# A causal convolution's taps: eight of 31 on TensorE, or fourteen of 31 on GpSimd

## The chip, the cores and the metric

The kernel runs on one core of one Trainium2 chip. The metric is the device time of one execution in microseconds; of several executions the median is given.

## What is computed

Two stacked networks on 256 tokens of width 1024, in float32. The first has two layers of SwiGLU and mixer (pooling, then latent attention); the second has a mixer of three branches and a mixture of experts. The change touches the second network's mixer:

```python
o_a = dsa_attention(q_a, k_a, v_a, q_i, k_i, w_i, topk)              # 8 heads
o_b = conformer_conv(conv_in, conv_w[l], conv_b[l], ln_g[l], ln_b[l])
o_m = memory_attention(q_m, mem, g_mem[l], w_mem_kv[l], g_qm[l], g_km[l])   # 4 heads
merged = (gates[:, :, 0] * (o_a @ w_br_a[l]) + gates[:, :, 1] * (o_b @ w_br_b[l])
          + gates[:, :, 2] * (o_m @ w_br_m[l]))
x = x + merged @ w_o[l]

def conformer_conv(conv_in, conv_w, conv_b, ln_g, ln_b):
    a, gte = jnp.split(conv_in, 2, axis=-1)
    u = a * jax.nn.sigmoid(gte)                       # (256, 512)
    y = depthwise causal convolution of u, 31 taps, + conv_b
    return jax.nn.silu(layernorm(y, ln_g, ln_b))
```

## The kernel before

The program is written out by hand for five engines, and its order is the order of the code; semaphores join the engines. Weights stream from HBM in blocks of 128 rows into a ring `raw`. Each block is split in two parts of reduced precision, `uh` on ScalarE (L449) and `ul = raw - uh` on VectorE (L460), and TensorE multiplies each block three times (L524 to L526), once with each useful pair of parts. The activations are split alike into `hh`/`hl` or `bh`/`bl`.

Steps of other work are put between the blocks: `later` holds generators that give a step at each `unit_done`, by a budget; `flush` runs what is left. So the heads of the two attentions run beside the gates' blocks: eight heads `qa`, then four heads `qm`. A head is turned, scored, its maximum taken on VectorE (`heads_dve`, L1783 or L1787), its exponential on ScalarE (L1754), then turned and multiplied (L1702, L1715). `heads_dve` calls `extra` once per step, and `extra` issues four taps of the convolution.

The convolution works on columns: `uT` holds `u` turned, 4 groups of 128 channels by 286 positions, 30 of them zeros, copied from PSUM at L2596. The tap (k, j) is `uT[:, k, j:j+256]` times the column `cw[:, k, j]`. `cw` comes at L2681, from the rows that GpSimd loads as `conv_w`. The taps 0 to 22 of each group, 92 in all, are VectorE's: one instruction of 128x256 each (L2390 for the first, L2392 for the others) that adds into `yc`. All `arena` and `Gs` names in the rows of this line are SBUF tiles. The taps 23 to 30, 32 in all, are TensorE's: ScalarE makes a diagonal matrix from the identity and the tap's column (`taps_act`, L2400), and TensorE multiplies two 128x128 pieces of `uT` by it and adds up in two banks (`taps_pe`, L2409). Each of these float32 products is two records in the trace. Then TensorE adds `yc`, turned by a product with the identity (L2553), into the same banks. VectorE takes mean and variance (L2731, L2733), ScalarE and VectorE make the root (L802, L791 to L797), and VectorE writes the normed rows (L2740).

Around that stand the three branches (`branch_pe`). A branch has two column halves c of four input blocks k each. Branch 0 takes `o_a`, then branch 2 takes `o_m` (turned at L837, parts at L852 and L858), then branch 1 takes the convolution. Merges are on VectorE (L2488). The order on TensorE is: branch 0, flush of the heads `qm`, eight of its taps, the turn of `om`, 24 taps, the sum with `yc`, branch 2 with the turn of the normed rows at the start of its second half, branch 1.

GpSimd makes loads of its own queue (L3344, L691), the roots of some norms (L998, L1000), the division in the latent attention's softmax (L1956) and four small rows (L1584). After the load of `conv_w` it waits for the heads' end and issues eight loads for the router.

## Time and profile before

| | us |
|---|---|
| median of 3 runs (lowest, highest) | 1565.17 (1562.39, 1565.42) |
| the profiled execution, its own time | 1564.39 |
| its span in the profile | 1562.3 |
| TensorE busy | 1523.4 (98%) |
| VectorE busy | 1217.6 (78%) |
| ScalarE busy | 877.4 (56%) |
| GpSimd busy | 117.2 (8%) |
| DMA, mean share of 16 engines | 373.75 MB at 239 GB/s |

The span is that of the profiled execution; 2.1 us of its time lie around it. "PE" in the rows is TensorE's products, "PEld" its weight loads, "DVE" VectorE, "ACT" ScalarE, "POOL" GpSimd. Products overlap, so the step from one start to the next tells what a row of products costs, not the duration of one. In a timeline row, `x4` with a time means four instructions in a row within that time.

### The profile page before, as it was taken

What the parts mean: (1) busy time and instruction counts of PE and PEld (TensorE: products, weight loads), DVE (VectorE), ACT (ScalarE), POOL (GpSimd) and SP (SyncE); (2) the same over time, 40 slices, a digit from 0 to 9 for tenths busy, and PEclk for the clock granted to TensorE, in tenths of its full rate; (3) what the DMA queues carried; (4) which work ended last, traced back from release to release, by engine and by line L of the source; (5) the groups of instructions that cost most, each with busy time, mean ns of one, the idle gap of its engine ahead of it and who ended that gap; (6) DMA issues with size and microseconds to landing.
All of it is one profiled execution on the core that took longest, in us unless ns stands there. A gap on an engine that the chain in (4) does not pass through costs nothing.

```text
span 1562.3 us, 19111 instructions
## 1 busy us (share of the span) xinstructions
PE 1523.4 (98%) x7361; PEld 1218.0 (78%) x7361; DVE 1217.6 (78%) x1782; ACT 877.4 (56%) x1349; POOL 117.2 (8%) x180
## 2 busy tenths in 40 slices
PE   7999999999999999999999999999999999999997
PEld 4878876878878887766788887877788888787876
DVE  1898978988868888665585654669888798888996
ACT  2545436544447444377564544655567477777774
POOL 1110020000001000015211000000001000000000
PEclk9999999999999999999999999899999999999999
DMA  9999856988857988333286544445324479989893
GB/s 345 374 378 357 301 202 217 333 301 305 305 178 264 339 285 309 118 109 108 82 310 189 185 147 142 157 152 193 113 81 131 162 258 363 344 316 334 306 344 132
DMA packets 196400, 373.75 MB, mean 239 GB/s; under 512 B 9042, under 2 KB 102672, under 8 KB 196304
## 3 DMA queue, kind: packets, MB, share of 16 engines
q1 hardware_dynamic: 176688, 301.08, 55.8%
q0 software_dynamic: 18928, 69.77, 12.7%
q10 hardware_dynamic: 688, 1.62, 0.3%
q8 instruction: 60, 0.98, 0.2%
q14 instruction: 36, 0.29, 0.1%
HBM read 371.39 MB, written 1.05 MB: 238 GB/s over the span
## 4 chain that ended last, share of the span: by engine, by line
PE 89%; ACT 4%; DVE 4%; POOL 1%; DMA 1%; SPq 1%; issue 1%; DVEq 0%; ACTq 0%
PE banks L524 25%; PE banks L526 25%; PE banks L525 25%; PE banks L1165 1%; ACT arena L807 1%; ACT uh L449 1%; DVE ul L460 1%; PE banks L2409 1%; DMA raw<-in_ffn_w_in 1%; PE banks L3011 1%; PE banks L835 1%; PE banks L981 1%; PE banks L2018 1%; PE banks L1843 1%; PE banks L766 1%
## 5 line engine op out<-in xcount | busy, mean ns | idle before, releaser
L460 DVE TENSOR_TENSOR ul<-raw,uh 128x1024 fp32r<-128x1024 f32 (+2 forms) x548 | 657.1, 1209 | 156.3 <-ACT uh L449 147.2
L449 ACT ACTIVATE uh<-raw 128x1024 fp32r<-128x1024 f32 (+2 forms) x548 | 568.4, 1048 | 346.7 <-PE banks L526 342.4
L524 PE MATMUL banks<-uh,hh 128*128 128x512 f32 (+2 forms) x1296 | 517.4, 399 | 4.2 <-DVE ul L460 1.9
L526 PE MATMUL banks<-uh,hl 128*128 128x512 f32 (+2 forms) x1296 | 503.9, 389 | 0.0
L525 PE MATMUL banks<-ul,hh 128*128 128x512 f32 (+2 forms) x1296 | 503.0, 388 | 0.0
L524 PEld LDWEIGHTS banks<-uh,hh 128*128 128x128 f32 x1296 | 245.5, 189 | 60.3 <-issue 6.1
L526 PEld LDWEIGHTS banks<-uh,hl 128*128 128x128 f32 x1296 | 245.3, 189 | 51.1
L525 PEld LDWEIGHTS banks<-ul,hh 128*128 128x128 f32 x1296 | 245.9, 190 | 45.4 <-issue 0.2
L524 PE MATMUL banks<-uh,bh 128*128 128x512 f32 x512 | 207.3, 405 | 1.0 <-DVE bl L3208 0.9
L526 PE MATMUL banks<-uh,bl 128*128 128x512 f32 x512 | 200.0, 391 | 0.0
L525 PE MATMUL banks<-ul,bh 128*128 128x512 f32 x512 | 199.5, 390 | 0.0
L715 DVE SCALAR_TENSOR_TENSOR arena<-arena,sc 128x512 f32<-128x512 f32 x210 | 157.9, 752 | 9.9 <-DVE bl L1233 0.5
L524 PEld LDWEIGHTS banks<-uh,bh 128*128 128x128 f32 x512 | 96.1, 188 | 29.2 <-DVE bl L3208 6.2
L526 PEld LDWEIGHTS banks<-uh,bl 128*128 128x128 f32 x512 | 96.1, 188 | 20.9
L525 PEld LDWEIGHTS banks<-ul,bh 128*128 128x128 f32 x512 | 96.3, 188 | 20.0 <-issue 1.7
L691 POOL DMA_DIRECT2D arena<-in_ada_w x60 | 45.3, 755 | 472.5 <-DVE arena L715 397.9
L1215 ACT ACTIVATE sg<-banks 128x256 f32<-128x256 f32 x88 | 29.0, 380 | 62.0 <-PE banks L526 62.0
L2392 DVE SCALAR_TENSOR_TENSOR Gs<-arena,Gs 128x256 f32<-128x256 f32 x88 | 42.7, 485 | 3.2
L1248 DVE TENSOR_TENSOR ug<-sg,banks 128x256 f32<-128x256 f32 x88 | 33.0, 415 | 11.4 <-ACT sg L1215 11.3
L1233 DVE TENSOR_TENSOR bl<-banks,bh 128x512 fp32r<-128x512 f32 x44 | 30.1, 684 | 4.1 <-ACT bh L1203 4.1
L774 ACT ACTIVATE arena<-banks 128x128 f32<-128x128 f32 x20 | 5.6, 279 | 40.6 <-PE banks L751 40.6
L1203 ACT ACTIVATE bh<-banks 128x512 fp32r<-128x512 f32 x44 | 25.6, 582 | 4.3 <-PE banks L1165 4.3
(402 smaller groups left out, 1267.0 us busy)
## 6 DMA issues: line engine op xcount, KB each, us to landing
raw<-in_ffn_w_in SPq DMA_DIRECT2D x176, 512.0 KB, 6.7
raw<-in_w_up SPq DMA_DIRECT2D x64, 1024.0 KB, 6.5
arena<-in_ada_w POOLq DMA_DIRECT2D x60, 1024.0 KB, 7.4
raw<-in_ffn_w_out SPq DMA_DIRECT2D x44, 1024.0 KB, 5.7
raw<-in_w_down SPq DMA_DIRECT2D x32, 1024.0 KB, 6.2
raw<-in_w_in SPq DMA_DIRECT2D x22, 1024.0 KB, 5.0
raw<-in_ada_w SPq DMA_DIRECT2D x12, 1024.0 KB, 10.5
raw<-in_w_mem_kv SPq DMA_DIRECT2D x4, 1024.0 KB, 6.0
```

The costliest lines, as they stand in the source:

```text
L449: act.e.activation(uh[r][:, 0:w], raw[m % NRAW][:, h * w:(h + 1) * w], AF.Copy).then_inc(act_done, ta.put("hi", u))
L460: dve.e.tensor_tensor(ul[r][:, 0:w], raw[m % NRAW][:, h * w:(h + 1) * w], uh[r][:, 0:w].bitcast(F32), ALU.subtract).then_inc(dve_done, tv. ...
L524: pe.e.matmul(o, a, wh, start=k + j == s0, stop=False)
L525: pe.e.matmul(o, a, wl, start=False, stop=False)
L526: mm = pe.e.matmul(o, b, wh, start=False, stop=k + j == s1)
L691: pool.e.dma_start(ada_raw[m % NADA], v).then_inc(ada_ring[m % NADA], 16)
L715: dve.e.scalar_tensor_tensor(buf, w, sc[:, k:k + 1], buf, ALU.mult, ALU.add).then_inc(dve_done, tv.put())
L1203: act.e.activation(gT_h[b % 2][:, :, :], PB[6][:, :].rearrange("p (a b) -> p a b", b=S), AF.Copy).then_inc(act_done, ta.put("gh", q, b))
L1215: act.e.activation(sg[:, t, :], PB[up_banks(b)[t]][:, 0:256], AF.Silu).then_inc(act_done, ta.put("silu", q, b, t))
L1233: dve.e.tensor_tensor(gT_l[n][:, :, :], PB[6][:, :].rearrange("p (a b) -> p a b", b=S), gT_h[n][:, :, :].bitcast(F32), ALU.subtract).then_inc(
L1248: mul = dve.e.tensor_tensor(o, sg[:, t, :], u, ALU.mult)
L2392: tap = dve.e.scalar_tensor_tensor(y, u, w, y, ALU.mult, ALU.add)
```

## The change

GpSimd makes the taps 17 to 30 of each group (56), VectorE the taps 0 to 16 (68), and TensorE and ScalarE none. On GpSimd a tap is a product into `pt` (TENSOR_SCALAR) and an addition into `py` (TENSOR_TENSOR); the first four products go to `py` itself, so there are 56 products and 52 additions. Three products are issued ahead, and a product waits for the addition four places earlier in its buffer. VectorE adds `py` to `yc` (`taps_sum_dve`), and TensorE turns the sum into the two banks inside branch 0, before block 2 of its second half. The norm's root moves to GpSimd, by a power of -0.5. GpSimd's loads for the router stand behind that. The two new tiles take 8 KB of each partition, and the scratch for GpSimd's descriptors shrinks to 8192 bytes.

```diff
-PE_TAPS = 8
+POOL_TAPS = 14
+        py = sb("py", [P, 4, S])
+        pt = sb("pt", [P, 4, S])
...
-        def taps_act(act, taps, n):
...
-        def taps_pe(pe, taps, n):
...
+        def taps_pool(pool):
+            def product(i):
+                k, j = POOL_LIST[i]
+                o = py[:, k, :] if i < 4 else pt[:, i % 4, :]
                 if i >= 8:
+                    pool.wait_ge(pool_done, tg("tap", i - 4))
+                pool.e.tensor_scalar(o, uT[:, k, j:j + S], cw[:, k, j:j + 1], None, ALU.mult).then_inc(
+                    pool_done, tg.put("product", i))
+
+            pool.wait_ge(dve_done, tv("cw"))
+            pool.wait_ge(act_done, ta("uT", 2))
+            n = len(POOL_LIST)
+            for i in range(7):
+                product(i)
+            for i in range(4, n):
+                if i + 3 < n:
+                    product(i + 3)
+                y = py[:, i % 4, :]
+                pool.wait_ge(pool_done, tg("product", i))
+                if i < 8:
+                    pool.wait_ge(pool_done, tg("product", i - 4))
+                else:
+                    pool.wait_ge(pool_done, tg("tap", i - 4))
+                pool.e.tensor_tensor(y, y, pt[:, i % 4, :], ALU.add).then_inc(pool_done, tg.put("tap", i))
+
+        def taps_sum_dve(dve):
+            last = len(POOL_LIST) - 4
+            for k in range(4):
+                dve.wait_ge(pool_done, tg("tap", last + k))
+                dve.own()
+                dve.e.tensor_tensor(yc[:, k, :], yc[:, k, :], py[:, k, :], ALU.add).then_inc(
+                    dve_done, tv.put("conv", k))
...
+            def conv_out():
+                pe.later.flush("qm")
+                tp.same("ht")
...
+                for k in range(4):
+                    pe.wait_ge(dve_done, tv("conv", k))
+                    for t in range(T):
+                        mm = pe.e.transpose(PB[6 + t][:, k * P:(k + 1) * P], yc[:, k, t * P:(t + 1) * P], ident[:, :])
+                mm.then_inc(pe_done, tp.put("conv"))
...
+            branch_pe(pe, 0, lbh, lbl, parts_ready(pe, "oa"), mids={(1, 2): conv_out})
             turn_pe(pe, "om", 4, om_part, lambda: pe.wait_ge(dve_done, tv("o", "qm", 1, 0)))
-            taps_pe(pe, taps, 999)
...
-            act.wait_ge(dve_done, tv("ss", "ln"))
-            rstd_act(act, "ln", st[:, 50:52], 1)
...
+            merge_dve(dve, 0, 0)
+            dve.unit_done()
+            taps_dve(dve, taps, 999)
+            taps_sum_dve(dve)
+            split_low(dve, dve.unit_at + 1)
+            dve.unit_done()
+            dve.unit_done()
             dve.later.flush("qm")
             tv.same("ht")
-            taps_dve(dve, taps, 6)
-            split_low(dve, dve.unit_at + 3)
+            merge_dve(dve, 0, 1)
             plain_dve(dve, "om", 4, bh, bl)
-            taps_dve(dve, taps, 999)
             dve.wait_ge(pe_done, tp("conv"))
...
+            split_low(dve, dve.unit_at + 3)
+            for t in range(T):
+                dve.wait_ge(pool_done, tg("lnr", t))
...
             load("conv_w", cwr, I["conv_w_2"][0].rearrange("j a n -> j (a n)"))
+            taps_pool(pool)
+            for t in range(T):
+                r = st[:, 52 + t:53 + t]
+                pool.wait_ge(dve_done, tv("ss", "ln", t))
+                pool.e.tensor_scalar(r, st[:, 41 + 2 * t:42 + 2 * t], EPS, None, ALU.add).then_inc(pool_done, tg.put())
+                pool.wait_ge(pool_done, tg.n)
+                pool.e.tensor_tensor(r, r, minus_half, ALU.pow).then_inc(pool_done, tg.put("lnr", t))
...
-    nc = _bacc.Bacc("TRN2", target_bir_lowering=False, num_devices=1)
+    nc = _bacc.Bacc("TRN2", target_bir_lowering=False, num_devices=1, dynamic_dma_scratch_size=8192)
```

The lines of the changed kernel stand one further down up to 2390 or so, and about ten from there on. TensorE before, from the last step of the heads to the first product of branch 2; L524 to L526 are branch products, L1715 a head, L2409 the taps, L837 the turn of `om`, L2553 the sum:

```order
L1715 MATMUL banks<-kvm,Gs 128x128 x4
L524 MATMUL banks<-uh,bh 128x512
...
L526 MATMUL banks<-uh,bl 128x512
L2409 MATMUL banks<-arena 128x128 x16
L837 MATMUL banks<-ident,arena 128x128 x8
L2409 MATMUL banks<-arena 128x128 x48
L2553 MATMUL banks<-ident,Gs 128x128 x8
L524 MATMUL banks<-uh,bh 128x512
```

The same place now; L2567 is the turn of the sum:

```order
L1716 MATMUL banks<-kvm,Gs 128x128 x4
L2567 MATMUL banks<-ident,Gs 128x128 x8
L525 MATMUL banks<-uh,bh 128x512
...
L527 MATMUL banks<-uh,bl 128x512
L838 MATMUL banks<-ident,arena 128x128 x8
L525 MATMUL banks<-uh,bh 128x512
```

The taps are gone, and the sum stands in front of the last twelve products of branch 0 instead of behind the turn.

VectorE before, from the last head to the norm; L1787 and L1792 are a head's maximum, L2392 taps, L2488 a merge, L1798 and L1804 the heads' end, L858 low parts of `om`:

```order
L1787 TENSOR_REDUCE st<-banks 128x2
L1792 SCALAR_TENSOR_TENSOR st<-st 128x2
L2392 SCALAR_TENSOR_TENSOR Gs<-arena,Gs 128x256 x4
L2488 TENSOR_TENSOR arena<-arena,banks 128x512 x2
L2392 SCALAR_TENSOR_TENSOR Gs<-arena,Gs 128x256 x8
L2488 TENSOR_TENSOR arena<-arena,banks 128x512 x2
L1798 RECIPROCAL st<-st 128x8
L1804 TENSOR_TENSOR arena<-banks,st 128x512 x2
L2392 SCALAR_TENSOR_TENSOR Gs<-arena,Gs 128x256 x6
L460 TENSOR_TENSOR ul<-raw,uh 128x1024 x3
L858 TENSOR_TENSOR bl<-banks,bh 128x512 x2
L2392 SCALAR_TENSOR_TENSOR Gs<-arena,Gs 128x256 x14
```

Now; L2426 is the sum with GpSimd's taps, L2745 to L2751 the norm:

```order
L2393 SCALAR_TENSOR_TENSOR Gs<-arena,Gs 128x256 x4
L2503 TENSOR_TENSOR arena<-arena,banks 128x512 x2
L2393 SCALAR_TENSOR_TENSOR Gs<-arena,Gs 128x256 x4
L2426 TENSOR_TENSOR Gs<-Gs,py 128x256 x4
L461 TENSOR_TENSOR ul<-raw,uh 128x1024
L1799 RECIPROCAL st<-st 128x8
L1805 TENSOR_TENSOR arena<-banks,st 128x512 x2
L2503 TENSOR_TENSOR arena<-arena,banks 128x512 x2
L859 TENSOR_TENSOR bl<-banks,bh 128x512 x2
L2745 BN_STATS st<-banks 128x6
L2747 BN_AGGR st<-st 128x2
```

Of these 32 taps 24 are gone, four stay in front of the first merge and four behind it, and the four sums stand before the second merge. Two splits (L461) follow the statistics, ahead of the normed rows. GpSimd now, behind its load of the tap weights (before, the loads for the router came next):

```order
L3355 DMA arena<-in_conv_w 31x512
L2402 TENSOR_SCALAR py<-arena 128x256 x4
L2402 TENSOR_SCALAR pt<-arena 128x256 x4
L2419 TENSOR_TENSOR py<-py,pt 128x256
L2402 TENSOR_SCALAR pt<-arena 128x256
```

The last two rows then alternate up to the last four additions.

## Rows read from the trace of the kernel before

**Rows 1.** The page: busy time and share, and the chain by engine.
```profile
PE 1523.4 (98%) x7361; PEld 1218.0 (78%) x7361; DVE 1217.6 (78%) x1782; ACT 877.4 (56%) x1349; POOL 117.2 (8%) x180
...
PE 89%; ACT 4%; DVE 4%; POOL 1%; DMA 1%; SPq 1%; issue 1%; DVEq 0%; ACTq 0%
```

**Rows 2.** Busy time by stretches: from the tap weights to the sum's new place.
```profile
core 0: us, PE busy (x) PEld busy (x) DVE busy (x) ACT busy (x) POOL busy (x), PEclk, DMA share, GB/s
1073.50:1171.00 97.50, 96.85 (x502) 77.79 (x502) 83.99 (x158) 60.17 (x120) 0.00 (x0) 1.00 0.36 119
```

**Rows 3.** TensorE's timeline: start, us in all, what [idle before].
```profile
1170.95 0.48 PE L524 MATMUL banks<-uh,bh 128*128 128x512 f32 x1
...
1173.77 3.73 PE L2409 MATMUL banks<-arena 128*128 128x128 f32 x32
1177.34 1.04 PE L837 MATMUL banks<-ident,arena 128*128 128x128 f32 x8
1179.40 10.98 PE L2409 MATMUL banks<-arena 128*128 128x128 f32 x96 [1.03 <-ACT arena L2400]
1190.33 2.27 PE L2553 MATMUL banks<-ident,Gs 128*128 128x128 f32 x16
1192.36 0.48 PE L524 MATMUL banks<-uh,bh 128*128 128x512 f32 x1
...
1197.91 1.03 PE L837 MATMUL banks<-ident,arena 128*128 128x128 f32 x8
```

**Rows 4.** ScalarE's timeline: the turned input, and the parts of `om`.
```profile
1069.92 1.07 ACT L2596 ACTIVATE arena<-banks 128x512 f32<-128x512 f32 x2
...
1177.98 1.09 ACT L852 ACTIVATE bh<-banks 128x512 fp32r<-128x512 f32 x2 [5.52 <-PE banks L837]
```

**Rows 5.** VectorE's timeline: the tap weights, the last taps, the norm, the router's weights.
```profile
1073.16 0.28 DVE L2681 COPY arena<-banks 128x124 f32<-128x124 f32 x1
...
1167.68 4.13 DVE L2392 SCALAR_TENSOR_TENSOR Gs<-arena,Gs 128x256 f32<-128x256 f32 x8
...
1195.98 1.53 DVE L2740 TENSOR_SCALAR arena<-banks,st 128x512 f32<-128x512 f32 x2
...
1233.05 0.45 DVE L2757 TENSOR_TENSOR arena<-arena,cc 128x288 f32<-128x288 f32 x1
```

**Rows 6.** VectorE's timeline at two places of the first network.
```profile
477.40 0.42 DVE L1096 TENSOR_TENSOR hl<-full,hh 128x256 fp32r<-128x256 f32 x1
477.74 1.22 DVE L460 TENSOR_TENSOR ul<-raw,uh 128x1024 fp32r<-128x1024 f32 x1
...
676.01 1.02 DVE L460 TENSOR_TENSOR ul<-raw,uh 128x832 fp32r<-128x832 f32 x1
```

**Rows 7.** GpSimd's groups by form: busy us, mean ns | idle before.
```profile
L1956 POOL TENSOR_SCALAR full<-full,st 128x256 f32<-128x256 f32 x16 | 14.6, 925 | 7.5 <-DVE st L1923 7.5
...
L1584 POOL TENSOR_TENSOR arena<-arena 4x256 f32<-4x256 f32 x2 | 1.5, 730 | 1.4 <-DMA arena<-in_pool_scale 1.3
```

**Rows 8.** GpSimd's timeline: the norms' roots, and the first load for the router.
```profile
468.00 0.30 POOL L998 TENSOR_SCALAR st<-st 128x1 f32<-128x1 f32 x1 [47.10 <-ACT arena L807]
468.39 0.57 POOL L1000 TENSOR_TENSOR st<-st 128x1 f32<-128x1 f32 x1
...
478.50 0.63 POOL L998 TENSOR_SCALAR st<-st 128x1 f32<-128x1 f32 x1 [3.56 <-ACT arena L807]
...
676.76 0.43 POOL L998 TENSOR_SCALAR st<-st 128x1 f32<-128x1 f32 x1 [3.56 <-ACT arena L807]
...
1177.42 0.55 POOL L3344 DMA_DIRECT2D Gs<-in_g_ffn  x1 [196.86 <-DVE Gs L2392]
```

**Rows 9.** VectorE's groups by form from 1073.5 to 1171 us.
```profile
L2392 DVE SCALAR_TENSOR_TENSOR Gs<-arena,Gs 128x256 f32<-128x256 f32 x67 | 32.5, 485 | 2.4
L460 DVE TENSOR_TENSOR ul<-raw,uh 128x1024 fp32r<-128x1024 f32 x21 | 25.4, 1222 | 6.8 <-ACT uh L449 6.5
...
L1636 DVE TENSOR_TENSOR Gs<-arena 128x320 f32<-128x320 f32 x2 | 1.0, 494 | 0.1
```

More of the change, by code:

```diff
@@ L370, in build @@
         cwr = om[0:CONVW, 0, :]
-        dg = [v[:, t, h * P:(h + 1) * P] for v in (mask, score) for t in range(T) for h in range(2)]
         grow = ht
@@ L2393, in taps_dve @@
                 tap.then_inc(dve_done, tv.put("tap", k, j))
-        def taps_act(act, taps, n):
-            for i, (k, j) in taps.some(n):
-                act.wait_ge(dve_done, tv("o", "qa", 1, 0))
+        def taps_pool(pool):
+            def product(i):
+                k, j = POOL_LIST[i]
+                o = py[:, k, :] if i < 4 else pt[:, i % 4, :]
                 if i >= 8:
-                    act.wait_ge(pe_done, tp("tap", i - 8))
-                act.e.activation(dg[i % 8], ident[:, :], AF.Copy, scale=cw[:, k, j:j + 1]).then_inc(
-                    act_done, ta.put("dg", i))
-        def taps_pe(pe, taps, n):
-            for i, (k, j) in taps.some(n):
-                pe.wait_ge(act_done, ta("dg", i))
-                for t in range(T):
-                    if i == 0:
-                        pe.take(6 + t)
-                    mm = pe.e.matmul(PB[6 + t][:, k * P:(k + 1) * P], uT[:, k, j + t * P:j + (t + 1) * P], dg[i % 8],
-                                     start=(i == 0), stop=False)
-                mm.then_inc(pe_done, tp.put("tap", i))
+                    pool.wait_ge(pool_done, tg("tap", i - 4))
[23 more added lines that the diff above has]
+                    dve_done, tv.put("conv", k))
         gsel, gbias = gb[:, 512:518], gb[:, 0:512]
@@ L2542, in mix_pe @@
                 pe, "oa", 4, om_part, lambda: pe.wait_ge(dve_done, tv("o", "qa", 1, 0)), bk=OA_BANKS))
-            branch_pe(pe, 0, lbh, lbl, parts_ready(pe, "oa"))
-            pe.later.flush("qm")
-            tp.same("ht")
-            taps = Taps(PE_LIST)
-            taps_pe(pe, taps, 8)
-            turn_pe(pe, "om", 4, om_part, lambda: pe.wait_ge(dve_done, tv("o", "qm", 1, 0)))
-            taps_pe(pe, taps, 999)
-            for k in range(4):
-                pe.wait_ge(dve_done, tv("tap", k, CONVW - PE_TAPS - 1))
-                for t in range(T):
-                    mm = pe.e.matmul(PB[6 + t][:, k * P:(k + 1) * P], yc[:, k, t * P:(t + 1) * P], ident[:, :],
-                                     start=False, stop=(k == 3))
-            mm.then_inc(pe_done, tp.put("conv"))
-            for t in range(T):
-                pe.frees(6 + t, dve_done, tv, "ln", t)
+            def conv_out():
+                pe.later.flush("qm")
+                tp.same("ht")
+                for t in range(T):
+                    pe.take(6 + t)
+                for k in range(4):
[4 more added lines that the diff above has]
+                for t in range(T):
+                    pe.frees(6 + t, dve_done, tv, "ln", t)
+            branch_pe(pe, 0, lbh, lbl, parts_ready(pe, "oa"), mids={(1, 2): conv_out})
+            turn_pe(pe, "om", 4, om_part, lambda: pe.wait_ge(dve_done, tv("o", "qm", 1, 0)))
             def ln_turn():
```

21 lines of the change are left out of this document (6 added, 15 removed).

## The prediction

> **What bounds the kernel now.** I read the page first. TensorE is busy for 98% of the span and GpSimd for 8%, and TensorE holds 89% of the chain that ended last [rows 1]. So time is won where TensorE has fewer instructions on that chain, and lost where it is made to wait. Then I read the table by stretches for the part that the change touches. Between 1073.5 us, when the turned tap weights are there, and 1171 us, when TensorE has done two of the four input blocks of the second half of branch 0, TensorE is busy for 96.85 of 97.5 us, VectorE for 83.99, ScalarE for 60.17, and GpSimd not at all; the granted clock is 1.00, TensorE's upper level of 2.4 GHz [rows 2]. TensorE sets the pace there, and VectorE has 13.5 us to spare. Third, TensorE's timeline: behind branch 0 come 32 tap products from 1173.77, the turn of `om`, a wait, 96 tap products from 1179.40, the 16 products of the sum, and branch 2 from 1192.36 [rows 3]. Last, I looked at what GpSimd and VectorE do to each other, since the change puts the two beside each other.
>
> **What the change takes from TensorE.** The 32 PE taps (two matmuls each, shown as 128 records) go. Start to start they take 1177.34 - 1173.77 = 3.57 us and 1190.33 - 1179.40 = 10.93 us: 14.5 us [rows 3], all on the path. The sum's products stay (1192.36 - 1190.33 = 2.0 us), moved into branch 0. The idle time in front of 1179.40 (1.0 us) is replaced by a wait for the high parts of `om`: ScalarE makes them in 1.09 us from 1177.98, right behind the turn [rows 4]. Branch 2 now stands there, so I count that as even. ScalarE also loses 32 products and, with the root, a table load: it idled 5.52 us before those high parts [rows 4], so this is worth nothing. From TensorE alone: **-14.5 us**.
>
> **What VectorE must do by then.** Its 68 taps are as many as it had done in the heads before: 4 first taps, then four per head step, and the four that I take from the group of eight that starts at 1167.68 [rows 5]; they end at 1167.68 + 4 x 0.516 (4.13 / 8) = 1169.75. New are four sums, 0.42 us each by a 256 wide addition [rows 6], so the sum is ready at about 1171.4, and TensorE, there at 1170.95 [rows 3], waits 0.5 to 1 us: **+0.7 us**. The 24 taps that VectorE loses (12.4 us) stood beside the 96 products and were not on the path. They are worth nothing.
>
> **GpSimd's own work.** The inputs are there early: the turned rows at 1069.92 + 1.07 us [rows 4], the weights at 1073.16 + 0.28 = 1073.44 [rows 5]. GpSimd then issues 56 products and 52 additions of 128x256. A product is a TENSOR_SCALAR of that very size, 0.925 us; the nearest addition row is a TENSOR_TENSOR of 4x256, 0.730 us [rows 7]. The program has a wait for the addition in front of nearly every product, and such a step costs 0.39 - 0.30 = 0.09 us [rows 8]. With 56 x 0.925 + 52 x (0.73 + 0.09) = 51.8 + 42.6 I get **94 us**: alone it would be done at 1167.8, before VectorE's last tap. If nothing disturbs it, it is hidden.
>
> **The disturbance.** Here the trace speaks against the change. A 128x1 TENSOR_SCALAR on GpSimd takes 0.30 us (468.00). Twice it was longer in the rows shown (and once more, alike, at 781): 0.63 us from 478.50 and 0.43 from 676.76 [rows 8]. Each time VectorE was in the split L460, which reads `raw` and `uh`, both in SBUF: until 478.96 and 677.03 [rows 6]. GpSimd ended at 479.13 and 677.19, so each time 0.16 or 0.17 us behind VectorE's end. That isn't a share of a bandwidth; GpSimd stood still until VectorE was through. Of the reverse, VectorE held by a reading GpSimd, the trace has no case: VectorE has no instruction with two SBUF inputs beside the 32 products of 0.92 us in the latent attention [rows 7]. I take it that the wait goes both ways, because what makes one of two engines wait for the other's whole instruction is most simply one thing that either can hold.
>
> Price: 0.30 us of a GpSimd instruction is there even for one column [rows 8], so a product reads for 0.925 - 0.30 = 0.625 us and an addition for 0.43. In all 56 x 0.625 + 52 x 0.43 = 57 us, 0.53 on average. VectorE's instructions with two SBUF inputs in the stretch are 67 taps (32.5 us), 21 splits (25.4), 12 steps of the rotation (six lines like the one shown, 6.0) and 3 short ones for the norms (1.3): 103 instructions, 65 us [rows 9]. VectorE's other 19 us cover about 19 / 0.83 = 22 GpSimd instructions. The other 86 each push VectorE back by 0.53 us: 46 us. VectorE's 13.5 us of spare time take up a part, so it ends 32 us late. One GpSimd instruction for each of VectorE's also means that GpSimd ends no later than VectorE. TensorE needs VectorE in every head (the maxima) and for every split, and has 0.65 us of idle time: it is late by the same **+32 us**. Bounds: if everything packs perfectly, 65 + 57 = 122 us have to fit in 97.5, which is +25; if an instruction holds for its whole length, 65 + 90 = 155, which is +57. I take 32, since the 0.30 us row is GpSimd's own overhead and is near.
>
> The Trainium skill, page "SBUF — State Buffer", section "Who interferes with whom", has a rule on just this: a VectorE instruction with two SBUF inputs contends with a GpSimd instruction that reads SBUF, and whichever starts first holds the shared ports for its whole instruction. The held rows agree with it in one direction, and no row here shows the other. By that rule to the letter the wait would be the upper bound, +57, and the sum +44.
>
> **Behind the sum.** The norm's root moves to GpSimd: 0.30 + 0.57 us per row block plus the step between (0.09) [rows 8], in place of ScalarE's table load and VectorE's four small steps. From the sum's end TensorE has 2.8 us of branch 0, 0.9 of the turn, 1.1 of waiting and 5.5 of branch 2 (1197.91 - 1192.36 [rows 3]) before it wants the normed rows, 10.3 us. VectorE needs until then a merge, low parts, two statistics, two splits and the two normings (1.53 us [rows 5]): about 11.3 us. **+1.0 us**. GpSimd's eight loads for the router now stand behind the roots. They took 5 us to issue from 1177.42 [rows 8] and are wanted at 1233 [rows 5]; even 40 us of lateness shifts both alike. The smaller descriptor scratch I cost at nothing, since GpSimd sits idle before nearly every load; if that cover fails, a load starts a few us later in the first half of the kernel.
>
> **Sum.** -14.5 + 0.7 + 32 + 1.0 = +19.2 us on the profiled execution's 1564.39: 1583.6. The median of the runs is 0.8 above the profiled one, so I forecast **1584 us**. With the bounds of the wait, 1577 (+25) to 1609 (+57).
>
> **Rivals.** (a) No disturbance: GpSimd is done at 1167.8 and only -14.5 + 0.7 + 1.0 = -12.8 remains, 1552. For it: no row shows VectorE held. Against it: the held instructions [rows 8]. Faster. (b) Only GpSimd waits, VectorE never: behind each VectorE instruction it gets one in, and with waits of about 0.2 us in each of 103 it ends some 20 us after 1167.8, so TensorE waits about 16 us at the sum: +3, 1568. For it: the rows show just this direction. The point from which it decides is a GpSimd end after 1171 with VectorE on time. (c) VectorE always goes first and GpSimd gets only the remainder, 97.5 - 65 = 32 us, or 39 instructions; the other 69 take 59 us alone, so TensorE waits at one place until 1230: +59 - 13 = +46, 1611. (d) The change doesn't do what it says: the order of instructions shows that it does, so no chance of its own.
>
> **Numbers.** Forecast 0.5, (a) 0.27, (b) 0.13, (c) 0.1. Since (a) is above 0.2 the range must hold it; it leaves out (c) and the top of the forecast's own bounds: 1551 to 1602. The likeliest case's own range is 1577 to 1609. 0.2%, some 3 us, is about what a measurement of this kernel can tell from no change: faster is (a) and a little of (b), 0.28; the same is half of (b), 0.08; slower is the rest, 0.64.
>
> **What would show it.** L2393 and L461 on VectorE, 485 and 1222 ns now, get longer or get idle time in front of them by about half a us each; the 56 products average above 925 ns; the stretch from the weights to the sum lasts about 130 us instead of 97.5; TensorE's busy share in it falls to about three quarters, with waits spread over all heads. Right behind it 14.5 us are gone. If VectorE's means stay and GpSimd ends before TensorE reaches the sum, (a) is right and I am wrong in the disturbance; one long wait of TensorE before L2567 would be (b) or (c).

## The result and the profile after

| | before, measured beside it | after |
|---|---|---|
| median, us (lowest, highest) | 1564.09 (1562.37, 1565.42) | 1574.26 (1572.48, 1576.81) |
| ratio (95% interval) | | 1.0073 (1.0062 to 1.0084) |
| profiled execution, own time / span | 1564.39 / 1562.3 | 1576.81 / 1575.2 |

Slower by 10.2 us, where 19.2 were forecast. The profiled execution of after is the slowest of its six, so differences of spans (12.9) are some 3 us above those of medians.

The page of after, busy time and chain by engine, answers to [rows 1]:

```profile
PE 1513.7 (96%) x7225; PEld 1206.4 (77%) x7225; DVE 1222.2 (78%) x1756; ACT 866.4 (55%) x1315; POOL 236.2 (15%) x292
...
PE 80%; POOL 8%; DVE 5%; ACT 3%; issue 1%; DMA 1%; SPq 1%; DVEq 0%; ACTq 0%
```

GpSimd had 1% of the chain and now has 8%; TensorE fell from 89 to 80. So the path went over to GpSimd somewhere. The table by stretches answers to [rows 2]: first from the tap weights (1074.50) to the end of the heads, then two stretches behind TensorE's wait:

```profile
1074.50:1178.00 103.50, 98.58 (x501) 78.72 (x501) 96.86 (x155) 59.30 (x113) 99.45 (x88) 0.98 0.33 112
...
1193.40:1196.00 2.60, 2.19 (x8) 1.17 (x9) 2.30 (x4) 0.00 (x0) 1.44 (x2) 0.50 0.00 0
1196.00:1200.00 4.00, 4.00 (x16) 3.23 (x15) 2.19 (x4) 0.00 (x0) 0.00 (x0) 0.73 0.53 156
```

In the first row VectorE is busy for 96.86 us, where it was 83.99, and TensorE still for 95% of the time: the heads are 5.8 us longer (TensorE is at the sum 103.3 us after the weights instead of 97.5), not 32. The granted clock is 0.50 behind the wait, TensorE's lower level of 1.2 GHz. TensorE's timeline, answering to [rows 3]:

```profile
1177.03 1.05 PE L1716 MATMUL banks<-kvm,Gs 128*128 128x128 f32 x8
1193.44 0.69 PE L2567 MATMUL banks<-ident,Gs 128*128 128x128 f32 x2 [15.37 <-DVE Gs L2426]
1194.31 0.69 PE L2567 MATMUL banks<-ident,Gs 128*128 128x128 f32 x2 [0.18 <-DVE Gs L2426]
...
1199.86 1.03 PE L838 MATMUL banks<-ident,arena 128*128 128x128 f32 x8
...
1202.13 0.50 PE L525 MATMUL banks<-uh,bh 128*128 128x512 f32 x1 [1.23 <-DVE bl L859]
```

One wait of 15.4 us before the sum. Who is late is told by VectorE's timeline, answering to [rows 5]:

```profile
1174.81 2.43 DVE L2393 SCALAR_TENSOR_TENSOR Gs<-arena,Gs 128x256 f32<-128x256 f32 x4
1192.46 3.19 DVE L2426 TENSOR_TENSOR Gs<-Gs,py 128x256 f32<-128x256 f32 x4 [15.22 <-POOL py L2419]
...
1204.49 2.33 DVE L461 TENSOR_TENSOR ul<-raw,uh 128x1024 fp32r<-128x1024 f32 x2
1206.73 1.52 DVE L2751 TENSOR_SCALAR arena<-banks,st 128x512 f32<-128x512 f32 x2
```

VectorE is through with its taps at 1177.24 and idles for 15.2 us, released by GpSimd's addition. GpSimd's timeline from there, with the roots of the norm:

```profile
1189.10 0.92 POOL L2402 TENSOR_SCALAR pt<-arena 128x256 f32<-128x256 f32 x1
1189.99 0.72 POOL L2419 TENSOR_TENSOR py<-py,pt 128x256 f32<-128x256 f32 x1
1190.81 0.92 POOL L2402 TENSOR_SCALAR pt<-arena 128x256 f32<-128x256 f32 x1
1191.70 3.13 POOL L2419 TENSOR_TENSOR py<-py,pt 128x256 f32<-128x256 f32 x4
1203.71 0.22 POOL L3425 TENSOR_SCALAR st<-st 128x1 f32<-128x1 f32 x1 [8.88 <-DVE st L2747]
1204.02 0.57 POOL L3427 TENSOR_TENSOR st<-st 128x1 f32<-128x1 f32 x1
1204.67 1.09 POOL L3425 TENSOR_SCALAR st<-st 128x1 f32<-128x1 f32 x1
1205.84 1.38 POOL L3427 TENSOR_TENSOR st<-st 128x1 f32<-128x1 f32 x1
```

GpSimd worked from 1074.61 to 1194.84: 120.2 us where I had 94. The second pair of roots takes 1.09 and 1.38 us instead of 0.22 and 0.57; it stands beside the two splits of 1204.49. Last the groups, VectorE's to 1178 answering to [rows 9], GpSimd's to [rows 7]:

```profile
L2393 DVE SCALAR_TENSOR_TENSOR Gs<-arena,Gs 128x256 f32<-128x256 f32 x64 | 41.6, 650 | 2.3
L461 DVE TENSOR_TENSOR ul<-raw,uh 128x1024 fp32r<-128x1024 f32 x21 | 26.1, 1254 | 0.9 <-ACT uh L450 0.9
...
L1793 DVE SCALAR_TENSOR_TENSOR st<-st 128x2 f32<-128x2 f32 x12 | 3.4, 287 | 0.4
...
L2391 DVE TENSOR_SCALAR Gs<-arena,cc 128x256 f32<-128x256 f32 x4 | 2.4, 590 | 0.1
```

```profile
L2402 POOL TENSOR_SCALAR pt<-arena 128x256 f32<-128x256 f32 x52 | 62.8, 1209 | 4.7
L2419 POOL TENSOR_TENSOR py<-py,pt 128x256 f32<-128x256 f32 x52 | 48.1, 928 | 0.0
L2402 POOL TENSOR_SCALAR py<-arena 128x256 f32<-128x256 f32 x4 | 6.1, 1539 | 93.1 <-DVE arena L2692 93.1
```

Both engines are held by the other: a tap on VectorE went from 485 to 650 ns, a product on GpSimd from 925 to 1233 (68.9 us / 56), an addition from 0.72 (its length behind 1178, with VectorE idle) to 928.

Where the 12.9 us between the spans are: tap weights later +1.1 (in runs 1 and 3 below, with the same code up to there, they are ready at 1070.6, so this is scatter of the first network), heads +5.8, from their end to the sum +15.6 (the wait), taps of TensorE -14.5, the rest up to branch 2 (the half clock, the handing over of `om`) +1.8, branch 2 to the turn in its middle +0.9, behind it +2.2.

### The profile page after: what moved, and what is told of

Its sections match the earlier page's. It is cut to its first block, busy times and chain, and to the rows that moved or that the text cites. A ratio compares the mean times of both kernels' runs of the same rounds, so it can differ in the third digit from the quotient of the medians.

```text
span 1575.2 us, 18895 instructions
## 1 busy us (share of the span) xinstructions
PE 1513.7 (96%) x7225; PEld 1206.4 (77%) x7225; DVE 1222.2 (78%) x1756; ACT 866.4 (55%) x1315; POOL 236.2 (15%) x292
## 3 DMA queue, kind: packets, MB, share of 16 engines
HBM read 371.39 MB, written 1.05 MB: 236 GB/s over the span
## 4 chain that ended last, share of the span: by engine, by line
PE 80%; POOL 8%; DVE 5%; ACT 3%; issue 1%; DMA 1%; SPq 1%; DVEq 0%; ACTq 0%
PE banks L525 24%; PE banks L527 23%; PE banks L526 23%; POOL pt L2402 4%; POOL py L2419 3%; DVE ul L461 2%; PE banks L1166 1%; ACT arena L808 1%; ACT uh L450 1%; DMA raw<-in_ffn_w_in 1%; PE banks L3022 1%; PE banks L836 1%; PE banks L982 1%; PE banks L2019 1%; PE banks L1844 1%
## 5 line engine op out<-in xcount | busy, mean ns | idle before, releaser
L461 DVE TENSOR_TENSOR ul<-raw,uh 128x1024 fp32r<-128x1024 f32 (+2 forms) x548 | 658.0, 1211 | 150.1 <-ACT uh L450 141.6
L526 PE MATMUL banks<-ul,hh 128*128 128x512 f32 (+2 forms) x1296 | 504.5, 389 | 0.0
L526 PEld LDWEIGHTS banks<-ul,hh 128*128 128x128 f32 x1296 | 246.8, 190 | 45.7 <-issue 0.2
L526 PE MATMUL banks<-ul,bh 128*128 128x512 f32 x512 | 200.0, 391 | 0.0
L526 PEld LDWEIGHTS banks<-ul,bh 128*128 128x128 f32 x512 | 96.6, 189 | 19.9 <-issue 1.7
L2402 POOL TENSOR_SCALAR pt<-arena 128x256 f32<-128x256 f32 x52 | 62.8, 1209 | 4.7
L2419 POOL TENSOR_TENSOR py<-py,pt 128x256 f32<-128x256 f32 x52 | 48.1, 928 | 0.0
L999 POOL TENSOR_SCALAR st<-st 128x1 f32<-128x1 f32 x16 | 5.5, 347 | 268.1 <-ACT arena L808 268.1
```

The lines of the kernel that those rows point to most:

```text
L461: dve.e.tensor_tensor(ul[r][:, 0:w], raw[m % NRAW][:, h * w:(h + 1) * w], uh[r][:, 0:w].bitcast(F32), ALU.subtract).then_inc(dve_done, tv. ...
L526: pe.e.matmul(o, a, wl, start=False, stop=False)
L2402: pool.e.tensor_scalar(o, uT[:, k, j:j + S], cw[:, k, j:j + 1], None, ALU.mult).then_inc(pool_done, tg.put("product", i))
L2419: pool.e.tensor_tensor(y, y, pt[:, i % 4, :], ALU.add).then_inc(pool_done, tg.put("tap", i))
```

## The experiments

The time of each run is compared with the kernel before as measured beside that run (medians of 1561.8 to 1563.2 us), and two runs are compared by their differences from it. In runs 1, 2, 3, 5 and 6 the result of the convolution is incomplete or wrong, since GpSimd's share is left out or replaced.

Theory when they began: VectorE and GpSimd hold each other (but for less than forecast), and GpSimd's late end makes the wait. Rival: GpSimd is just slow, or something else in the changed order is.

**1. GpSimd's taps left out**

```diff
-            taps_pool(pool)
...
-                dve.wait_ge(pool_done, tg("tap", last + k))
...
-                dve.e.tensor_tensor(yc[:, k, :], yc[:, k, :], py[:, k, :], ALU.add).then_inc(
+                dve.e.tensor_tensor(yc[:, k, :], yc[:, k, :], yc[:, k, :], ALU.max).then_inc(
```

> GpSimd's 108 instructions are left out, and the four sums on VectorE take the maximum of yc with itself, so the result lacks the taps 17 to 30; all else is the changed kernel. Theory (the two engines hold each other up at a shared read of SBUF, and the sum then waits for GpSimd): with no GpSimd work VectorE's taps take 485 ns again, the splits 1222, TensorE reaches the sum 6 us sooner and doesn't wait 15 us there: 1574 - 6 - 15 = 1553 us, which is also the 1552 that I gave for no disturbance. Rival (the loss lies in the new order: the sum inside branch 0, the norm's root on GpSimd behind its own queue): the sum's 15 us go, but VectorE's 6 us of lateness stay: 1559 us or more.

Measured: 1547.78 us, 0.9911 (0.9894 to 0.9928) of before, 5 us below the expectation. VectorE's groups have their old lengths:

```profile
L2393 DVE SCALAR_TENSOR_TENSOR Gs<-arena,Gs 128x256 f32<-128x256 f32 x64 | 31.0, 485 | 2.3
L461 DVE TENSOR_TENSOR ul<-raw,uh 128x1024 fp32r<-128x1024 f32 x25 | 30.2, 1221 | 6.8 <-ACT uh L450 6.6
```

TensorE's timeline at the sum shows no wait, 97.6 us after the weights (1070.57):

```profile
1168.15 1.04 PE L2566 MATMUL banks<-ident,Gs 128*128 128x128 f32 x8
...
1171.77 1.03 PE L838 MATMUL banks<-ident,arena 128*128 128x128 f32 x8
```

So everything that the change costs comes from GpSimd's 108 instructions and the wait for them: 10.2 us above the kernel before with them, 15.4 below it without, 25.6 in all. It also shows a price that I did not have: from the sum to the turn of `om` it is 3.6 us here and 6.4 in the changed kernel (1193.44 to 1199.86), where the granted clock is 0.50 and 0.73, against 1.00 here. The wait costs TensorE 2.8 us more than its own length; 0.4 of them are two more short waits, and the other 2.4 go with the lower clock.

**2. GpSimd works, nobody waits for it at the sum.** As 1, but with `taps_pool`.

> GpSimd makes all its 108 instructions, but the four sums on VectorE don't read or await them (they take the maximum of yc with itself), so the result lacks the taps 17 to 30. Theory: the disturbance stays and only the wait at the sum goes. VectorE's taps keep their 650 ns mean in the heads, TensorE is about 6 us late there, and the norm's root on GpSimd now has to queue behind the unfinished taps: GpSimd's end stays near 1194 us, the roots come behind it, and the turn of the normed rows waits for them, about 10 us. So 1574 - 15 + 5 to 10 = 1564 to 1569 us. Rival (VectorE is not held by GpSimd but by something in the order of its own work): GpSimd's instructions are as long as alone (0.92 and 0.73 us) once nothing waits for them.

Measured: 1568.04 us, 1.003 (1.0018 to 1.0041). The groups are as in the changed kernel (taps 651 ns), and TensorE is at the sum after 103.4 us. So the 5.8 us in the heads are VectorE's lateness alone, and no effect of the wait. But of the wait's 15.4 us only 5.4 came back in the time (10.2 above the kernel before with it, 4.8 without). TensorE's waits tell why:

```profile
PE banks L838 <- DVE arena L2750: 8.1, 1, 8.1
PE banks L1703 <- ACT Gs L1765: 3.8, 4, 1.5
```

The second line is 3.8 us in the changed kernel too and 0.2 in run 1: it is the lateness in the heads. L2750 is the normed rows, which need the root, and the root stands behind the last addition on GpSimd (1196.63 us there). GpSimd's late end is paid at the next place that needs the engine.

**3. The same number of writes without a read.** Each product and addition becomes a MEMSET of 128x1024 that waits for the one before; the sums wait for the last four, but don't read them.

```diff
-                pool.e.tensor_scalar(o, uT[:, k, j:j + S], cw[:, k, j:j + 1], None, ALU.mult).then_inc(
-                    pool_done, tg.put("product", i))
+                pool.wait_ge(pool_done, tg.n)
+                pool.e.memset((py if i < 4 else pt)[:, :, :], 0.0).then_inc(pool_done, tg.put("product", i))
...
-                pool.e.tensor_tensor(y, y, pt[:, i % 4, :], ALU.add).then_inc(pool_done, tg.put("tap", i))
+                pool.wait_ge(pool_done, tg.n)
+                pool.e.memset(py[:, :, :], 0.0).then_inc(pool_done, tg.put("tap", i))
```

> GpSimd's 56 products and 52 additions are replaced by 108 MEMSETs of 128x1024 into pt and py, each waiting for the one before, and the sums don't read py but still wait for the last four; the result lacks the taps 17 to 30. GpSimd then writes as much as it can and reads nothing. Theory (only a GpSimd instruction that reads SBUF holds up VectorE's second input): VectorE's taps are back at 485 ns and its two-column instruction of a head at 161 ns, while GpSimd is busy beside them. Rival (any GpSimd work, or its writes, holds VectorE up): taps stay above 550 ns and the two-column instruction above 200.

Measured: 1561.32 us (one run). GpSimd is busy for 108 x 0.955 = 103.1 us within 109.3, and VectorE's groups read:

```profile
L2393 DVE SCALAR_TENSOR_TENSOR Gs<-arena,Gs 128x256 f32<-128x256 f32 x64 | 31.0, 485 | 2.3
L461 DVE TENSOR_TENSOR ul<-raw,uh 128x1024 fp32r<-128x1024 f32 x22 | 26.6, 1222 | 6.8 <-ACT uh L450 6.5
...
L2391 DVE TENSOR_SCALAR Gs<-arena,cc 128x256 f32<-128x256 f32 x4 | 4.0, 988 | 0.1
```

A GpSimd that is busy and writes does nothing to taps and splits; the one that makes products and additions does. The four first taps L2391 are the surprise: one input, and 988 ns instead of 414 (run 1) beside writes. The time is still 13.5 us above run 1: TensorE is 1.9 us later at the end of the heads (the four L2391 take 2.3 us more), it waits 7.2 us and three times 0.3 at the sum, because 109.3 us of MEMSETs end behind VectorE's taps, and comes to the turn of `om` 8.3 us after the start of the sum instead of 3.6. A GpSimd chain that is too long costs time without disturbing a tap.

**4. The smaller descriptor scratch alone**, in the kernel before.

```diff
-    nc = _bacc.Bacc("TRN2", target_bir_lowering=False, num_devices=1)
+    nc = _bacc.Bacc("TRN2", target_bir_lowering=False, num_devices=1, dynamic_dma_scratch_size=8192)
```

> The kernel before with nothing changed but the descriptor scratch of 8192 bytes. I costed that at nothing: 1564 us, ratio 1.000 within 0.1%. Rival (GpSimd's loads of the first network start later, which would explain that the changed kernel reaches the tap weights 1.1 us later than the kernel before): +1 us, 1565.

Measured: 1563.02 us, 1.0002 (0.9993 to 1.0012). Nothing, as costed.

**5 and 6. Only one-input, only two-input instructions on GpSimd.** I had priced a hold as the instruction's length less 0.30 us, which makes the product (0.625) worse than the addition (0.43).

```diff
-                pool.e.tensor_tensor(y, y, pt[:, i % 4, :], ALU.add).then_inc(pool_done, tg.put("tap", i))
+                pool.e.tensor_scalar(y, pt[:, i % 4, :], cw[:, 0, 0:1], None, ALU.mult).then_inc(pool_done, tg.put("tap", i))
```

```diff
-                pool.e.tensor_scalar(o, uT[:, k, j:j + S], cw[:, k, j:j + 1], None, ALU.mult).then_inc(
+                pool.e.tensor_tensor(o, uT[:, k, j:j + S], uT[:, k, 0:S], ALU.add).then_inc(
```

> All 108 GpSimd instructions read one array of SBUF (the additions are replaced by the multiplication of the product slot by a scalar, written to the sum; GpSimd's share of the convolution is wrong). My step in the prediction took a hold as an instruction's length less 0.30 us, so products (0.925 us, hold 0.625) would disturb more than additions (0.73 us, hold 0.43): VectorE's taps would have a mean over 650 ns, about 700. Theory now: a product holds VectorE's reads for about 0.2 us only and an addition for 0.5: taps' mean 530 to 590 ns, the two-column instructions near 161, and the sum place of TensorE reached about 100 us after the weights. GpSimd ends later than in the changed kernel either way (108 x 0.93 is 100 us alone, with VectorE's holds 120 to 130).

> All 108 GpSimd instructions read two arrays of SBUF (the products are replaced by additions of two stretches of the input; GpSimd's share is wrong). Theory now: additions hold VectorE for about 0.5 us each and come every 0.8 us: taps' mean 720 to 850 ns, two-column instructions 350 or more, splits over 1270. GpSimd ends about 90 to 100 us after the weights, so that the wait at the sum is under 3 us. Rival (hold is length less 0.30 us, products the worse): taps' mean 600 to 650 ns.

Measured, one run each: 1581.67 and 1575.94 us. The groups to 1178 us, first of only products, then of only additions:

```profile
L2393 DVE SCALAR_TENSOR_TENSOR Gs<-arena,Gs 128x256 f32<-128x256 f32 x64 | 34.2, 534 | 2.3
L461 DVE TENSOR_TENSOR ul<-raw,uh 128x1024 fp32r<-128x1024 f32 x22 | 27.9, 1276 | 4.5 <-ACT uh L450 4.5
```

```profile
L2393 DVE SCALAR_TENSOR_TENSOR Gs<-arena,Gs 128x256 f32<-128x256 f32 x48 | 39.0, 812 | 1.7
L461 DVE TENSOR_TENSOR ul<-raw,uh 128x1024 fp32r<-128x1024 f32 x21 | 34.4, 1650 | 0.0
```

Products cost a tap 49 ns, additions 327: the order is the reverse of mine. And the greater loss goes to the other side in each: with products alone GpSimd needs 128.8 us (104 by its steps of 0.96 us where VectorE is idle) and TensorE waits 27.5 us at the sum; with additions alone GpSimd is done in 104.2 us (89 by the steps of 0.82 us in the changed kernel), and VectorE is so late that the sum comes at 1196.29, with no wait there and TensorE's waits in the heads. So both of the cases that I weighed against each other exist, by the kind of instruction on GpSimd. Of the theory's numbers two were missed: GpSimd's 104.2 us with additions, where 90 to 100 were expected, and VectorE's two-column instructions, 184 ns with products instead of 161. The two kinds differ in two things, the operation and the number of arrays that GpSimd reads, and no run parts them: that it is the second array that makes an addition dear is argued, not shown.

Single collisions can be read from the changed kernel's timelines. Here are rows of GpSimd and VectorE by their starts, in windows narrow enough to hold one instruction:

```profile
1117.10 0.97 POOL L2402 TENSOR_SCALAR pt<-arena 128x256 f32<-128x256 f32 x1
1117.32 0.58 DVE L2393 SCALAR_TENSOR_TENSOR Gs<-arena,Gs 128x256 f32<-128x256 f32 x1
1118.05 0.97 POOL L2419 TENSOR_TENSOR py<-py,pt 128x256 f32<-128x256 f32 x1
1118.46 0.85 DVE L2393 SCALAR_TENSOR_TENSOR Gs<-arena,Gs 128x256 f32<-128x256 f32 x1
1119.12 2.03 POOL L2402 TENSOR_SCALAR pt<-arena 128x256 f32<-128x256 f32 x1
1119.22 1.21 DVE L461 TENSOR_TENSOR ul<-raw,uh 128x1024 fp32r<-128x1024 f32 x1
```

A tap takes 0.485 us undisturbed. The one that starts while a product is under way takes 0.58, the one that starts while an addition is under way 0.85; all 18 taps of that second sort in the changed kernel take 0.83 to 0.85, and in run 5, with products alone, none of the 64 taps takes more than 0.73. The other way round the product of 1119.12 is not done until 0.7 us behind the end of the split (1120.43): it waited for the tap before and for the whole split. The addition of 1118.05 waited for the end of a tap at 1118.42 and ended 0.60 us behind it. So either kind waits for the end of the VectorE instruction that is under way, a product makes the next tap wait for about 0.1 us (0.25 at most in run 5), and an addition for about 0.35. (Four taps of 1.05 us are an exception: an addition that started 0.04 us behind each of them was not held, and the tap was. Why is open.)

**7 and 8. Twelve taps on GpSimd, nineteen on VectorE**; then also the sum behind the turn of `om` (on VectorE the last taps, a split and the four sums move along with it).

```diff
-POOL_TAPS = 14
+POOL_TAPS = 12
```

```diff
-            branch_pe(pe, 0, lbh, lbl, parts_ready(pe, "oa"), mids={(1, 2): conv_out})
+            branch_pe(pe, 0, lbh, lbl, parts_ready(pe, "oa"))
...
             turn_pe(pe, "om", 4, om_part, lambda: pe.wait_ge(dve_done, tv("o", "qm", 1, 0)))
+            conv_out()
```

> GpSimd makes 12 taps, VectorE 19: 16 fewer GpSimd instructions, and 8 more taps on VectorE. Theory (GpSimd is the bound, 120.2 us for 108 instructions, and VectorE's sum place is reached at 1177 in the changed kernel): GpSimd ends 1.1 us x 16 = 18 us earlier, about 1177; VectorE's taps end 8 x 0.6 = 5 us later, about 1182; the sum at about 1183 instead of 1193, time 1564 to 1566. Rival (disturbance of VectorE is the cost, as I predicted, and moves with its load): VectorE with more taps ends later still, and the time stays at 1570 or more.

> As with 12 taps on GpSimd, but the sum stands behind the turn of the memory heads' output on TensorE and on VectorE, so that the last rows of the heads cover the end of the taps. Theory: the wait at the sum shrinks by the 2 to 4 us of the turn, 1560 to 1564. Rival (the sum is on the path wherever it stands, since the turn is short and needs VectorE, which is behind its taps): no better than with 12 taps alone.

Measured: 1562.12 us, 0.9999 (0.999 to 1.0009), and 1561.46, 0.9994 (0.9984 to 1.0004): level with the kernel before. VectorE's timeline with twelve taps:

```profile
1173.76 8.08 DVE L2393 SCALAR_TENSOR_TENSOR Gs<-arena,Gs 128x256 f32<-128x256 f32 x12
1181.95 2.01 DVE L2426 TENSOR_TENSOR Gs<-Gs,py 128x256 f32<-128x256 f32 x4
```

The sums start right behind the taps: GpSimd was done at 1180.5, and now VectorE is the bound; TensorE's wait is 5.4 us. The better balance brings 10.6 us (10.2 above the kernel before, now 0.5 below it), where 8 to 10 were expected. GpSimd's 92 instructions, 80 us without disturbance by the reckoning of the prediction, took 107.0, so it ended 3.5 us later than expected. Run 8 came out inside its expectation, but by its rival: at the later place the wait doesn't shrink, it is 6.5 us, since VectorE comes to the sum only after a merge, two splits and the low parts of `om`, and the 0.7 us between the two runs are inside their scatter.

**9. Two taps back on TensorE**: 12 on GpSimd, 17 on VectorE, the sum late as in 8.

```diff
-POOL_TAPS = 14
+PE_TAPS = 2
+POOL_TAPS = 12
...
-DVE_TAPS = [(k, j) for j in range(CONVW - POOL_TAPS) for k in range(4)]
+DVE_TAPS = [(k, j) for j in range(CONVW - POOL_TAPS - PE_TAPS) for k in range(4)]
+PE_LIST = [(k, j) for j in range(CONVW - POOL_TAPS - PE_TAPS, CONVW - POOL_TAPS) for k in range(4)]
...
+            taps_act(act, Taps(PE_LIST), 8)
...
             def conv_out():
+                taps_pe(pe, Taps(PE_LIST), 999)
```

> 12 taps on GpSimd, 17 on VectorE, 2 on TensorE by diagonal products (the way of the kernel before, 8 diagonal matrices from ScalarE), sum behind the turn of the memory heads' output. Theory (with 12 taps on GpSimd VectorE is the bound: its taps and what stands behind them keep TensorE waiting 6.5 us at the sum): two taps less take 8 x 0.65 = 5 us from VectorE, and the 16 products of TensorE (3.6 us) run inside its wait: the sum can start about 1183 instead of 1187, GpSimd being done at about 1180; 1556 to 1558, the first version under the kernel before by more than 0.2%. Rival (GpSimd's end at 1180, or the products added to TensorE, give it back): 1560 or more.

Measured: **1556.52 us, 0.9964 (0.995 to 0.9978)**, 5.2 us below the kernel before and inside the expectation. TensorE's timeline:

```profile
1178.01 3.74 PE L2413 MATMUL banks<-arena 128*128 128x128 f32 x32
1182.80 2.30 PE L2585 MATMUL banks<-ident,Gs 128*128 128x128 f32 x16 [1.05 <-DVE Gs L2447]
```

The tap products fill what was a wait, and no half clock follows: the granted clock is 1.00 from 1178 to 1190 us.

**10. The splits moved behind the normed rows**, in the changed kernel.

> The changed kernel with the two splits of the next weights moved behind the normed rows, so that nothing of VectorE stands beside GpSimd's four one-column root instructions. Theory: these take 0.22 and 0.57 us each instead of 0.5 and 0.7 (1.6 to 1.8 us less for the four), the normed rows start about 1.5 us earlier, but TensorE works on other branches then, so that the time changes by less than 1 us. Rival (the norm's rows are on the path): 1.5 us or more faster.

Measured: 1575.14 us, 1.0088 (1.0072 to 1.0103), not to be told from the changed kernel. GpSimd's second pair of roots is short again, and TensorE's waits have a new line:

```profile
1202.85 0.23 POOL L3425 TENSOR_SCALAR st<-st 128x1 f32<-128x1 f32 x1
1203.16 0.55 POOL L3427 TENSOR_TENSOR st<-st 128x1 f32<-128x1 f32 x1
```

```profile
PE banks L525 <- DVE ul L461: 2.4, 1, 2.4
```

The normed rows come earlier, the weights' low parts later: TensorE waits 2.4 us for them, where it was 0.6. What the roots gain the splits give back here.

**11. One tap on TensorE, VectorE's first tap made by ScalarE** beside it.

```diff
+                act.wait_ge(dve_done, tv("cw"))
+                act.wait_ge(act_done, ta("uT", 2))
+                for k in range(4):
+                    act.e.activation(yc[:, k, :], uT[:, k, 0:S], AF.Identity, scale=cw[:, k, 0:1],
+                                     bias=col("conv_b_2", k)).then_inc(act_done, ta.put("tap0", k))
```

> 12 taps on GpSimd, 18 on VectorE, 1 on TensorE (8 products); the first tap of VectorE's share, with the bias, is made by ScalarE in four activations instead (2.4 us off VectorE, 0.59 us each beside GpSimd). Theory (in the version with 17 taps on VectorE and 2 on TensorE the wait at the sum is down to 1.1 us, so that TensorE is the bound): VectorE has as much as in that version, TensorE 8 products of 0.23 us = 1.9 us less: 1554.5 to 1556. Rival (VectorE's and GpSimd's ends are the bound there already): the wait at the sum grows by the 1.9 us that TensorE saves, and the time stays at 1556.5, or ScalarE's four activations delay a head and it is slower.

Measured: 1562.14 us, 1.0003 (0.9994 to 1.0012): a miss by 6. ScalarE's and TensorE's timelines at the new place:

```profile
1069.29 2.08 ACT L2637 ACTIVATE Gs<-arena,cc 128x256 f32<-128x256 f32 x4 [2.49 <-DVE arena L2719]
```

```profile
1072.84 1.28 PE L2468 MATMUL banks<-gb 128*128 128x512 f32 x2 [4.23 <-ACT arena L2478]
1073.92 0.63 PE L527 MATMUL banks<-uh,hh 128*128 128x512 f32 x1
```

The four activations wait for the tap weights, with a split and the parts of a gate queued behind them, and TensorE waits 4.2 us for those and then works with steps of 0.43 instead of 0.23 us up to 1078, at a granted clock of 0.50. At the sum it waits for 2.8 us instead of the 1.1 of run 9. (The profiled execution, 1559.52 us, is the fastest of its eleven.) ScalarE is idle for 44% of the span, but its queue is in order: where a wait stands counts, not its idle share. The rival in the expectation named this at its end. Whether the four behind the gate would do better was not tried.

**12. The root alone on GpSimd**, in the kernel before.

```diff
-            act.wait_ge(dve_done, tv("ss", "ln"))
-            rstd_act(act, "ln", st[:, 50:52], 1)
...
+                pool.wait_ge(dve_done, tv("ss", "ln", t))
+                pool.e.tensor_scalar(r, st[:, 41 + 2 * t:42 + 2 * t], EPS, None, ALU.add).then_inc(pool_done, tg.put())
+                pool.wait_ge(pool_done, tg.n)
+                pool.e.tensor_tensor(r, r, minus_half, ALU.pow).then_inc(pool_done, tg.put("lnr", t))
```

> The kernel before, with the norm's root alone moved to GpSimd (two one-column instructions a tile, and the router's loads on GpSimd's queue behind them), taps, sum and splits as before. My step: +1.0 us on the path for the hand-over to GpSimd and its 0.22 and 0.57 us, against the hand-over to ScalarE. With the rows behind it free (no split beside it) 1563 to 1565. Rival (the norm is not on the path, TensorE has other branches): no difference, within 0.5 us of the kernel before.

Measured: 1561.56 us, 0.9998 (0.9988 to 1.0007). The rival holds: no difference.

## Why the prediction was right, and where its working was not

It gave slower, 1584 in a range of 1551 to 1602; it came to 1574.3. The sign came from the disturbance, and run 1 against the changed kernel shows that it stood there for the right reason: 25.6 us hang on GpSimd's instructions and the wait for them. Run 3 shows that the taps' lateness goes with GpSimd instructions that read, and not with a busy or a writing GpSimd. But three steps failed (the price of a hold, the spare time, GpSimd's end), and the clock was left out. That the total is only 10 us off is in part luck: VectorE's lateness was put 26 us too high, and 15.6 us of wait and 2.8 behind it were missing. The 1574.3 lies under the forecast's own bounds of 1577 to 1609; the range holds it only because it was stretched down to rival (a), and it came out between the forecast and rival (b), 1568.

- **TensorE's -14.5.** Right. Without GpSimd's taps the time is 15.4 us below the kernel before (run 1), close to the 14.5. In the -12.8 that the prediction gave for no disturbance stood +0.7 and +1.0 besides, and both of these were nothing (no wait at the sum in run 1; run 12).
- **GpSimd's own 94 us.** Right as a time without disturbance: behind 1178, with VectorE idle, a pair takes 1.71 us by the starts 1189.10 and 1190.81; the sum used 0.925 + 0.82 = 1.745.
- **"I take it that the wait goes both ways."** Right: a tap went from 485 to 650 ns and a product from 925 to 1233. It was a step without a row, so this was a guess that came true, and rival (a), that VectorE isn't held, fell with it.
- **The price of a hold, 0.625 and 0.43 us, 0.53 on average.** Wrong in size and order. VectorE lost in the stretch 64 x 0.165 + 21 x 0.032 + 12 x 0.125 + 4 x 0.176 = 13.4 us, or 0.16 for each of the 86 GpSimd instructions, not 0.53. By runs 5 and 6 it is additions that cost VectorE (327 ns a tap, against 49 with products). A tap that meets a product waits for 0.1 us, one that meets an addition for 0.35: for the addition the 0.43 was near, for the product the 0.625 was six times too high. A length less an overhead does not give the hold.
- **"VectorE's 13.5 us of spare time take up a part."** I let all of it count. VectorE lost 13.4 us and TensorE came to the sum 5.8 us late, so 7.6 were absorbed; of these 5.6 are the idle time before the splits, 6.5 before and 0.9 now. The rest of the spare time lay where nothing could be moved into it.
- **"GpSimd ends no later than VectorE."** Wrong, and this is the step that turned the picture. I had the two alternate one for one; in fact GpSimd lost 17.1 us on its products and 10.7 on its additions, twice as much as VectorE, and it had 94 us of its own in 97.5. It ended 17.6 us after VectorE's last tap. Of the signs that I had named the longer means came, but not the stretch of 130 us (103.3), nor TensorE's busy share of three quarters (95%), nor the waits spread over the heads. The wait of 15.4 us at one place is what rival (b) described. Its 16 us came out by two errors of about 6 us that cancel: GpSimd lost 28 us and not some 20, and TensorE was 5.8 us late in the heads and not on time.
- **The clock behind a wait.** Not in the sum: 2.8 us between the sum and the turn (run 1 against after), 0.4 of them waits. The granted clock is 0.50 and then 0.73 there, and 1.00 in run 1.
- **Root +1.0, scratch 0, the router's loads 0.** Run 12: the root and the loads behind it cost nothing where the taps aren't in front of it. Run 10 frees the roots from the splits, and nothing is gained. Run 4: the scratch costs nothing. Run 2 shows the one way in which the root can matter: queued behind late taps.

So the disturbance cost 5.8 + 15.6 + 2.8 = 24.2 us up to the turn, where I had 32 spread over the heads. The total was 10 us off, and its shape was wrong: I would have looked for the cure at VectorE, while the first cure was to give GpSimd less (run 7, 10.6 us).

The Trainium skill, page "SBUF — State Buffer", section "Who interferes with whom", says that a VectorE instruction with two SBUF inputs contends with a GpSimd instruction that reads, not with one that only writes. Runs 1, 3, 5 and 6 agree (485 ns alone and beside writes, 534 and 812 beside reads). The same section of the Trainium skill says that `tensor_scalar` can enter modes that take both port pairs and then contends; L2391, 414 ns alone and 988 beside writes, agrees, though no run shows the mode. The page's section "SBUF: two separate sides" of the Trainium skill says that whichever engine starts first has the shared ports "for the whole instruction". With VectorE first the trace agrees (the product of 1119.12 waited for the whole split). With GpSimd first it does not: a tap waits for 0.1 us behind a product of 0.925 and for 0.35 behind an addition of 0.72. By that rule to the letter the prediction had +57 us; the stretch up to the sum grew by 5.8 + 15.6 = 21.4.

What stays open: why a GpSimd instruction holds a tap for less than its own length, and whether it is the second array or the operation that makes an addition hold longer than a product. The collisions are those that the kernel happens to have, none under control. That the half clock costs 2.4 us is read from two kernels that differ in more than the clock.

## What to carry to other kernels

Before giving work to an idle GpSimd beside a busy VectorE, count both engines' lengths with the disturbance on both sides, and leave GpSimd some 25% of the stretch free: here 94 us took 120, and the 80 us of twelve taps took 107, beside a VectorE that was busy for over nine tenths of the time. The share is a number to be tuned by which engine's last instruction releases the sum (14 taps: GpSimd 17.6 us behind; 12: VectorE 1.3 us behind), and what is left as a wait of TensorE is worth filling with TensorE's own way of doing the work (run 9). A long wait can cost more than its length (15.4 us, and 2.4 more at the lower clock behind it), and an engine with idle time still makes others wait if a wait is put in front of what they need (run 11).

## What was not expected of the hardware

- The kind of GpSimd instruction decides who pays more. With products, which read one array, it is GpSimd (108 instructions in 128.8 us instead of 104, taps +49 ns); with additions, which read two, it is VectorE (taps +327 ns, splits +430 ns, GpSimd done in 104.2 us instead of 89). A tap started in a product waits for 0.1 us, in an addition for 0.35.
- GpSimd's writes without a read leave two-input VectorE instructions alone (485 and 1222 ns), and more than double a one-input TENSOR_SCALAR from SBUF to SBUF (414 to 988 ns).
- Small instructions can suffer as much as large ones: the two-column L1793 went from 162 (run 1) to 287 ns on average, and a one-column root of GpSimd from 0.57 to 1.38 us beside a split.
- On GpSimd a TENSOR_SCALAR of 128x256 with a scalar for each partition takes 0.92 us and a TENSOR_TENSOR of the same size 0.72.
